# Local attention's normalisation moved behind the value product, with a turned block per pair, in a one-core hybrid layer kernel

## What is computed

```python
s_loc = einsum('bnqgrd,bnkgd->bngrqk', qb, kw) * scale      # own block and its neighbours, |q - k| <= 128
s_ctx = einsum('bnqgrd,bkgd->bngrqk', qb, ck) * scale       # 128 cached keys
p = softmax(concatenate([s_loc, s_ctx, s_sink], axis=-1))   # s_sink: one learned number per head
out = einsum(p[..., :L], vw) + einsum(p[..., L:L + Lc], cv)
```

## Time and profile before

| | |
|---|---|
| median of 3 runs | 3861.84 us (3857.78 to 3863.82) |
| the profiled execution | 3859.45 us, its span 3857.7 us |
| PE busy | 3656.6 us, 95% |
| DVE busy | 2597.9 us, 67% |
| ACT busy | 693.5 us, 18% |
| POOL busy | 1627.5 us, 42% |
| granted TensorE clock, mean | 0.979 |

### The profile page before, as it was taken

How to read it: one execution, slowest core, us unless ns; L and a number is a source line. 1 busy time by engine, 2 the same in 40 slices (tenths; PEclk the granted TensorE clock), 3 DMA queues, 4 the chain that set the end, 5 groups by cost and what they waited for, 6 DMA issues and landing times. The chain is left out here.

```text
span 3857.7 us, 39956 instructions
## 1 busy us (share of the span) xinstructions
PE 3656.6 (95%) x13726; PEld 2088.9 (54%) x13726; DVE 2597.9 (67%) x6024; ACT 693.5 (18%) x1571; POOL 1627.5 (42%) x1498
## 2 busy tenths in 40 slices
PE   5888899999999999999989897999999999999997
PEld 3455587655555555554455566765555555555543
DVE  7784899956666676676624749987777465565444
ACT  1242366200000000000013425661000000000000
POOL 0210265456666544444402004553767565444330
PEclk9989899999999999999999998999999999999999
DMA  6323135789999999999830122457999999899774
GB/s 271 101 84 121 39 116 161 261 318 394 375 377 375 371 382 373 376 369 364 353 128 2 63 110 64 145 161 277 402 410 409 390 336 372 341 354 359 292 298 157
DMA packets 365049, 1026.96 MB, mean 266 GB/s; under 512 B 30352, under 2 KB 132016, under 8 KB 364208
## 3 DMA queue, kind: packets, MB, share of 16 engines
q0 software_dynamic: 147456, 536.94, 36.4%
q1 hardware_dynamic: 118352, 436.07, 29.5%
q10 hardware_dynamic: 99040, 51.40, 4.8%
HBM read 965.07 MB, written 59.22 MB: 266 GB/s over the span
## 5 line engine op out<-in xcount | busy, mean ns | idle before, releaser
L1874 PE MATMUL ps<-colsT,arena 128*128 128x384 f32 x4096 | 1361.6, 487 | 6.6 <-DMA arena<-in_peer_ut 4.4
L1874 PEld LDWEIGHTS ps<-colsT,arena 128*128 128x128 f32 x4096 | 776.3, 190 | 587.8 <-issue 100.2
L1908 PE MATMUL ps<-arena 128*128 128x512 f32 x1536 | 676.5, 592 | 0.0
L1385 POOL DMA_INDIRECT proj<-in_peer_u,eidx x336 | 473.4, 1409 | 233.6 <-DVE modbc L1577 116.4
L1385 POOL DMA_INDIRECT proj<-in_peer_v,eidx x335 | 359.0, 1072 | 316.5 <-DVE colsT L1588 217.6
L1908 PEld LDWEIGHTS ps<-arena 128*128 128x128 f32 x1536 | 291.8, 190 | 345.2 <-issue 317.6
L1577 DVE CUSTOM_DVE_ANT_0 proj<-proj,rows 128x1024 f32<-128x1024 f32 x336 | 399.6, 1222 | 58.0 <-DMA proj<-in_peer_u,eidx 56.1
L1371 POOL TENSOR_SCALAR x<-iota,modbc 128x128 f32<-128x128 f32 x192 | 143.1, 762 | 679.2 <-ACT modbc L1703 546.5
L1588 DVE SCALAR_TENSOR_TENSOR colsT<-proj,modbc,colsT 128x1024 f32<-128x1024 f32 x330 | 409.8, 1285 | 16.3 <-DMA proj<-in_peer_v,eidx 16.2
L1385 POOL DMA_INDIRECT modbc<-in_peer_v,eidx x177 | 200.8, 1135 | 326.5 <-DVE colsT L1588 259.0
L1908 PE MATMUL ps<-arena,rows 128*128 128x512 f32 x768 | 338.0, 592 | 0.2 <-DMA arena<-in_peer_v 0.2
(11 more groups left out here) (292 smaller groups left out, 3663.0 us busy)
## 6 DMA issues: line engine op xcount, KB each, us to landing
arena<-in_peer_ut SPq DMA_DIRECT2D x256, 512.0 KB, 6.8
arena<-in_peer_v SPq DMA_DIRECT2D x256, 512.0 KB, 6.7
gmat_d<-arena ACTq DMA_DIRECT2D x24, 2048.0 KB, 9.3
arena<-gmat_d SPq DMA_DIRECT2D x64, 768.0 KB, 9.1
proj<-in_w_adaT SPq DMA_DIRECT2D x51, 512.0 KB, 9.1
modbc<-in_w_adaT SPq DMA_DIRECT2D x19, 512.0 KB, 9.0
rows<-in_w_adaT SPq DMA_DIRECT2D x18, 512.0 KB, 3.5
arena<-in_w_in SPq DMA_DIRECT2D x2, 4224.0 KB, 16.3
```

What stands on the lines that cost most here:

```text
L1385: pool.indirect_dma_start(ring[slots[at]], None, tab, bass.IndirectOffsetOnAxis(ap=eidx[:, b * SLOTS + q:b * SLOTS + q + 1], axis=0)).then ...
L1874: mm = pe.matmul(ps[:, 2 + j % 2, 0:ND], utab[:, j % UR, k], hT[:, k, NG:T], start=(k == 0), stop=(k == KT - 1))
L1908: mm = pe.matmul(ps[:, Y_BANKS[2 * d + c2], :], wT[j % CR][:, d * P:(d + 1) * P], vtab[:, j % VR, c2 * 512:(c2 + 1) * 512], start=(j == 0) ...
```

## The change

Local attention: the exponentials go to TensorE as they are. `scaled` is gone; `values` swaps its operands, so that the result has queries on partitions and both heads of the pair side by side. A new `scaled_rows` on ScalarE multiplies it there by the reciprocal of the denominator while it empties PSUM (128x64 for each head) into a new tile `ytok`, and a new `turn_y` on TensorE turns the pair's 128x128 block, which `copy_y` then copies. The loop has one step more.

Order: `scores(0)` and `gz` now stand ahead of the loop, `gq` is in SLOT1 of step 0, and `kc` is a late unit in SLOT2 of step 3, whose bank `gv0` takes next. The wait for `sw3` moves from `scores(0)` to `turn_probs(0)`. On VectorE `head_max(s)` stands ahead of `denominators(s - 1)`.

PEER: `root_steps` computes a product of three factors in one instruction where the operand has one column; `mean(4)` and `normed(4)` stand one step later, each behind that step's marks; and from the second block on `exps` has an Exp on one column ahead of its wait.

```diff
         for _ in range(3):
-            c.link(dve.tensor_tensor(zz, yy, yy, ALU.mult))
-            c.link(dve.tensor_tensor(zz, zz, hh, ALU.mult))
+            if zz.shape[1] == 1:
+                c.link(dve.scalar_tensor_tensor(out=zz, in0=yy, scalar=hh, in1=yy, op0=ALU.mult, op1=ALU.mult))
+            else:
+                c.link(dve.tensor_tensor(zz, yy, yy, ALU.mult))
+                c.link(dve.tensor_tensor(zz, zz, hh, ALU.mult))
...
-        UNITS = ("ak", "aq0", "aq1", "swk", "aq2", "sw0", "aq3", "sw1", "av", "sw2", "sw3", "kc",
-                 "gz", "gq", "log0", "gk", "log1", "p0", "p1", "gv0", "gv1", "gv2", "gv3", "gv4", "mod", "conv0", "conv1",
+        UNITS = ("ak", "aq0", "aq1", "swk", "aq2", "sw0", "aq3", "sw1", "av", "sw2", "sw3", "gz",
+                 "gq", "log0", "gk", "log1", "p0", "p1", "kc", "gv0", "gv1", "gv2", "gv3", "gv4", "mod", "conv0", "conv1",
                  "gt0", "gt1")
-        EARLY_UNITS = UNITS.index("kc") + 1
+        EARLY_UNITS = UNITS.index("gz") + 1
...
-        SLOT1 = {0: "gz", 1: "log0", 2: "log1", 3: "p1", 4: "gv0", 5: "gv1", 6: "gv2", 7: "gv3", 8: "gv4", 9: "conv0"}
-        SLOT2 = {0: "gq", 1: "gk", 2: "p0", 8: "mod", 9: "conv1", 19: "gt0", 20: "gt1"}
+        SLOT1 = {0: "gq", 1: "log0", 2: "log1", 3: "p1", 4: "gv0", 5: "gv1", 6: "gv2", 7: "gv3", 8: "gv4", 9: "conv0"}
+        SLOT2 = {1: "gk", 2: "p0", 3: "kc", 8: "mod", 9: "conv1", 19: "gt0", 20: "gt1"}
...
-        PSTEPS = NPAIR + 3
+        PSTEPS = NPAIR + 4
...
+        ytok = region(x, 1696, 2, P)
...
                         pe.wait_ge(u_act, ACT_AT["av"])
-                        pe.wait_ge(u_dve, DVE_AT["sw3"])
+                        pe.wait_ge(u_dve, DVE_AT["av"])
+                        pe.wait_ge(gla_landed, 48)
...
                 def turn_probs(p):
                     j, b = pairs_[p]
+                    if p == 0:
+                        pe.wait_ge(u_dve, DVE_AT["sw3"])
                     for g in range(2):
                         i = 2 * p + g
-                        pe.wait_ge(pn_ready, i + 1)
+                        pe.wait_ge(p_ready, i + 1)
...
-                            mm = pe.matmul(ps[g * HD:(g + 1) * HD, 4 + p % 2, 0:P], vv[:, g * HD:(g + 1) * HD], probT[i % 4][:, n],
+                            mm = pe.matmul(ps[:, 4 + p % 2, g * HD:(g + 1) * HD], probT[i % 4][:, n], vv[:, g * HD:(g + 1) * HD],
                                            start=(n == 0), stop=(n == len(keys[b]) - 1))
                     mm.then_inc(av_done, 1)
+
+                def turn_y(p):
+                    pe.wait_ge(y_rows, 2 * p + 2)
+                    pe.transpose(ps[:, 4 + p % 2, P:2 * P], ytok[:, p % 2], ident[:, :]).then_inc(y_turned, 1)
...
                     if 2 <= s <= NPAIR + 1:
                         values(s - 2)
+                    if 3 <= s <= NPAIR + 2:
+                        turn_y(s - 3)
...
-                def scaled(p):
-                    j, b = pairs_[p]
+                def scaled_rows(p):
                     act.wait_ge(rd_ready, p + 1)
+                    act.wait_ge(av_done, p + 1)
+                    if p >= 2:
+                        act.wait_ge(y_turned, p - 1)
                     for g in range(2):
                         i = 2 * p + g
-                        rows_ = prob[i % NP_][:, 0:len(keys[b])].rearrange("p n q -> p (n q)")
-                        act.activation(rows_, rows_, ACT.Copy, scale=den[:, i:i + 1]).then_inc(pn_ready, 1)
+                        hs = slice(g * HD, (g + 1) * HD)
+                        act.activation(ytok[:, p % 2, hs], ps[:, 4 + p % 2, hs], ACT.Copy, scale=den[:, i:i + 1]).then_inc(y_rows, 1)
 
                 def copy_y(p):
                     j, b = pairs_[p]
-                    act.wait_ge(av_done, p + 1)
+                    act.wait_ge(y_turned, p + 1)
...
                 for s in range(PSTEPS):
-                    if 1 <= s <= NPAIR:
-                        scaled(s - 1)
+                    if s >= 4:
+                        copy_y(s - 4)
+                    if 3 <= s <= NPAIR + 2:
+                        scaled_rows(s - 3)
                     if s < NPAIR:
                         exps(s)
                     evac(SLOT1.get(s))
                     gla_part(s)
-                    if s >= 3:
-                        copy_y(s - 3)
                     evac(SLOT2.get(s))
...
+                    if s < NPAIR:
+                        head_max(s)
                     if 1 <= s <= NPAIR:
                         denominators(s - 1)
-                    if s < NPAIR:
-                        head_max(s)
...
                         if step < G_STEPS:
                             scatter_rows(k - 1, step)
+                        if k == 1 and step == 1:
+                            mean(4)
+                        if k == 1 and step == 2:
+                            normed(4)
                         if k == 1 or step >= 1:
                             route(k, step)
-                        if k == 1 and step == 0:
-                            mean(4)
-                        if k == 1 and step == 1:
-                            normed(4)
...
                 def exps(k):
+                    if k >= 1:
+                        act.activation(stats[:, 60:61], ones[:, 0:1], ACT.Exp)
                     act.wait_ge(ex_in, k + 1)
```

More of the change, by code:

```diff
@@ L198, in build @@
     sc_half = sem("sc_half")
+    y_rows, y_turned = sem("y_rows"), sem("y_turned")
     dots_ready, gelu_ready, coef_ready = sem("dots_ready"), sem("gelu_ready"), sem("coef_ready")
@@ L753, in filler @@
                 def filler(n):
-                    if n == "gz":
-                        columns(n, w_b, 0, 32)
+                    if n == "kc":
+                        free(n)
+                        pe.transpose(ps[:, banks(n)[0], 0:P], akT[:, 1], ident[:, :]).then_inc(u_mm, 1)
                     elif n == "gq":
@@ L806, in _ @@
                 swapped("sw3")
-                free("kc")
-                pe.wait_ge(u_dve, DVE_AT["ak"])
-                pe.transpose(ps[:, banks("kc")[0], 0:P], akT[:, 1], ident[:, :]).then_inc(u_mm, 1)
-                pe.wait_ge(gla_landed, 48)
+                scores(0)
                 pe.wait_ge(wb_landed, 16)
+                columns("gz", w_b, 0, 32)
                 for s in range(PSTEPS):
-                    if s < NPAIR:
+                    if 1 <= s < NPAIR:
                         scores(s)
@@ L892, in copy_y @@
                         dst = mixT[:, 4 + j, b * P:(b + 1) * P]
-                    act.activation(dst, ps[:, 4 + p % 2, 0:P], ACT.Copy).then_inc(yt_sb, 1)
+                    act.activation(dst, ps[:, 4 + p % 2, P:2 * P], ACT.Copy).then_inc(yt_sb, 1)
                 def gla_part(s):
```

## The result

| | before | changed | ratio |
|---|---|---|---|
| median, us | 3860.18 (8 runs, 3855.81 to 3863.82) | 3869.26 (8 runs, 3866.49 to 3877.17) | 1.0026 [1.0016, 1.0036] |
| profiled execution, us | 3859.45, span 3857.7 | 3866.49, span 3864.7 | |
| TensorE busy, us | 3656.6 | 3680.8 | |
| granted clock, mean | 0.979 | 0.974 | |

Forecast were 3854.8 us and a range of 3844 to 3867. The profiled executions are 7.0 us apart with the sign turned round: -7.0 was forecast, +7.0 came. The eight executions of the changed kernel go from 3866.49 us at a granted clock of 0.974 to 3877.17 at 0.969, and the profiled one is the shortest.

What follows compares the result with a forecast made beforehand. TensorE, busy 95% of the span, was taken as the bound. Mixers +2.3 (layer 0) and +1.4 (layer 1) and PEER heads -10.7 made -7.0 us, from the median of 3861.84 to 3854.8 us; range 3844 to 3867.

Steps and rivals of the forecast that it cites:

- 1. The start: Start of the mixer's pairs: scores(0) no longer waits for sw3; -4.6 us from step 2 in layer 0, -3.3 in layer 1.
- 2. The price of a pair: Mixer's value products +0.045 us a matmul, turned blocks 0.12 us each; together 7.8 us a layer, bounds 4.8 and 15.
- 3. kc: Layer 0 mixer: gv0 waits for VectorE's late kc copy, shrinking the 4.6 us gain to 0.8 by conv0; layer 1, 0.2.
- 4. The softmax wait: Mixer: turn_probs stops waiting for scaling; layer 0 +0.5, +0.8, +1.1, -1.2 us; layer 1 +3.4, +0.8, -1.3, +1.1, -1.2.
- 5. The tail: Mixer's end, before the projection: an extra round trip, +1.6 us, and +0.3 for a clock that may fall; +1.9 a layer.
- the round trip of 1.6: Mixer's end: ScalarE empties gt1, copies and scales, TensorE turns, before the projection can start; +1.6 us.
- 6. The head: PEER heads: shorter means and no VectorE idle before mean(4), less a clock fall; -5.4 us each, -10.7 for both.
- B: Rival, mixer steps 9 to 20: turn_y waits for ScalarE, 0.9 us for each of 24 pairs; +14.6, 3876.4 us; chance 0.12.
- C: Rival, PEER head gives nothing but the shorter means, held by ScalarE's evictions or GpSimd's marks; +0.1, 3862 us; chance 0.15.
- D: Rival, mixer: value products get cheaper, going by their 64 moving columns; up to 33 us less, 3822; chance 0.02.
- E: Rival: the clock does not fall in the head, nor behind kc; -15 us, 3847; chance 0.04.
- A: The forecast itself, mixers and heads summed: -7.0 us, own range -15 to +1; chance 0.67.

Runs made afterwards that it cites:

- e13: Changed kernel with the old normalisation and VectorE's denominators ahead of the next pair's maxima again: 3838.46 us, ratio 0.9952 to the kernel before.
- e2: Kernel before with the PEER edits alone: 3846.61 us, ratio 0.9967 to the kernel before.
- e4: Kernel before with the normalisation moved alone, old start and order of maxima, no PEER edits: 3883.37 us, ratio 1.0063 to the kernel before.
- e15: Kernel before with the normalisation moved alone and both heads' values moved (128 columns): 3857.75 us, ratio 1.0001 to the kernel before.
- e5: Changed kernel with both heads' values moved (128 columns) in the value products, half of them unused: 3840.69 us, ratio 0.9960 to the kernel before.
- e7: Changed kernel with VectorE's two gating products moved from step 13 to steps 15 and 17: 3855.93 us, ratio 1.0004 to the kernel before.
- e3: Changed kernel with the value products' operands swapped back (64 columns loaded, 128 moved; output not the attention's): 3840.15 us, ratio 0.9949 to the kernel before.
- e6: Changed kernel with kc turned into free columns of the probabilities' bank in step 4: 3863.75 us, ratio 1.0020 to the kernel before.
- e9: Changed kernel with the normalisation alone undone, maxima still ahead of the denominators: 3866.00 us, ratio 1.0016 to the kernel before.
- e11: Changed kernel with 128 moved columns, kc aside, earlier copy of pair 17's probabilities, gating products on GpSimd: 3842.53 us, ratio 0.9952 to the kernel before.

## Why the prediction was wrong

**1. The start.** Right in kind, and more than forecast. gk started 7.1 us earlier (-5.0 said), and -4.5 was left at scores(2) (-4.6 said), since gk ran 11.52 us, partly at half clock, behind an idle of 3.92. In layer 1 gk came 5.4 us earlier, measured from the start of the layer's first projections (81.43 us after it instead of 86.81; -3.3 said). e13 against e2 prices the new start at -5.8 for both layers together, a difference inside their intervals.

**2. The price of a pair.** Two halves. At full clock it was too high: 0.215 us a matmul against 0.19, +0.025 instead of +0.045. The turned block cost about the 0.12 us said. The clock is the other half. **This is the step that failed:** "Together 7.8 us a layer", with the bounds 4.8 and 15, priced the new products at full clock and took for granted that the steps around them would keep the clock of the kernel before. The bound named half clock, the value did not, and nothing in it tied the clock to the products themselves. e4 against e15, which differ in the moved width alone, is the price of that link: 23.9 us for both layers, 12 a layer on top of the 7.8.

From the Trainium skill ("TensorE: Matmul & The Clock Gate", "Back-to-back issue gap") the prediction took the gap of a single matmul, which goes by the moving columns. It was rightly set aside: the same section says that in a stream of weight loads and matmuls both set the spacing. This case's traces agree: e5's 6 matmuls with 128 moved columns took 1.34 us (228.52 to 229.86), the changed kernel's with 64 took 1.29, and the old ones, with 64 loaded and 128 moved, 0.19 each. So the loaded columns weigh more than the moved ones here. The same page's section "HAM oscillation — how this bites in real kernels" has the clock fall over gaps in which TensorE idles. The falls at step 14 before and after did come behind idle, those in e7 and e3 did not.

**3. kc.** Right: gv0 at 187.80 (187.7 said), turned probabilities at 196.55 (197.0), conv0 -2.0 (-0.8). The wait is harmless, as e6 shows, because conv0 does not start earlier without it.

**4. The softmax wait.** Right that it goes, wrong in what followed. For steps 9 to 17 of layer 0 +2.4 was said; from conv0 to step 16 it was +7.6, of which 5.3 came between steps 14 and 16 at half clock. At step 19 the prediction had the limiter right, VectorE's copy of pair 17's probabilities: TensorE waited 4.85 us for it (L1040). It started at 329.11 instead of 323.47, 5.6 us late, as late as the slow steps ahead had made the turned probabilities of step 16; the turned probabilities behind it were 4.2 late, so the -1.5 forecast came as -1.4.

**5. The tail.** From the turned probabilities of step 19 to the projection 14.28 us instead of 9.83: +4.5, where the surcharge of 1.4 and the round trip of 1.6, less the 1.1 us of the second wait, made +1.9. All of it ran at half clock. Another 2.1 us came behind it, as the projection began at half clock, for which the sum had 0.3.

**6. The head.** Mechanism right, size 1.2 us off for each head: no idle of 4 us before a mean, the second turn 5.7 and 6.0 us earlier from the head's start (7.0 said), and the third 4.2 and 4.1 instead of 5.4. A part of the difference is the mean, whose three Newton steps took 1.35 us instead of 1.74: 0.4 us less, where 0.6 was said. Timeline of TensorE:

```profile
546.87 0.47 PE L1901 MATMUL ps<-ident,proj 128*128 128x128 f32 x1 [2.96 <-DVEq L1486]
...
560.63 2.02 PE L1916 MATMUL ps<-x 128*128 128x128 f32 x16 [1.18 <-ACT arena L1751]
```

The 3 us of idle came as said, and so did their price: from this turn to the placing 13.76 us instead of 12.33 (541.79 to 554.12).

**The rivals.** B had the sign but not the cause: turn_y waited for ScalarE twice, 1.6 us in all, in the last step of each layer, and the value products waited four times for `copy_y`, 2.6 us. C, D and E did not happen. The case that came, pairs that stay at half clock, was spread over a bound of A and given no mechanism, no place and no chance. So the range ended 2 us below the measured median. The forecast's own upper bound of 15 us a layer would have made +7.4 in place of -7.0, but the range of A ended at +1.

**The sum, by the runs:** normalisation with the clock held +0.4, its clock +23.9, new start -5.8, PEER edits -12.7: +5.8, against +10.0 measured for all together. The difference of 4 lies within the intervals, which reach some 4 to 5 us each way, and the new start was priced with the old normalisation.

## What to carry to other kernels

Swapping a matmul's operands so that fewer columns move can make TensorE slow well beyond that matmul: before pricing it, look at the granted clock of the stages that it sits in, above all where it already falls, and put a price on half clock there. Where the load of the stationary operand sets the spacing, moving more columns costs next to nothing (0.223 us a matmul in e5 against 0.215), and unused ones can pay: e5 won 25 us with products that nobody reads. An edit that shortens one chain must be read with its partners: the maxima ahead of the denominators cost 25 us with the old normalisation (e9 against e13), whose scaling waits for the denominators before the probabilities are turned. With the new one no run prices them.

## What the runs showed that was not expected

- The clock fell at step 14 with no idle above 0.28 us in the 14 us ahead of it (e7, 64 moved columns), and at 269 us with none above 0.34 in the 7 us ahead (e3, 128 moved); low it stayed for 20 us in the one and 7 in the other.
- Doubling the value products' moved columns lowered TensorE's busy time by 20.7 us (3680.8 to 3660.1) through the clock.
- A VectorE operation on two columns took 2.86 us in place of 0.16 while GpSimd multiplied 128x1280 elements. The Trainium skill, "SBUF — State Buffer", section "SBUF: two separate sides", says that a VectorE operation with two inputs in SBUF and a GpSimd operation that reads SBUF exclude each other for a whole instruction; e11's trace agrees, with two stalls that end with GpSimd's products (265.30 and 268.26).
